# Gate/up bias loads on GpSimd's queue, the chunk count loaded once, and an output tail in quarters: a hybrid decoder step on one core

## What is computed

```python
x = x + merged @ w_out
hf = rmsnorm(x, g_ffn)
x = x + moe(hf, w_router, b_router, w_gu, b_gu, w_down, b_down)      # 32 experts, top 4
x = x + sigmoid(rmsnorm(x, g_ple) @ w_ple_gate) * (ple @ w_ple)

def expert(xblk, e):                        # D_FF = D_MODEL = 1024
    gu = xblk @ w_gu[e] + b_gu[e]           # 2 x 1024 columns: gate, up
    gate = minimum(gu[:, :D_FF], 7.0)
    up = clip(gu[:, D_FF:], -7.0, 7.0)
    hmid = (up + 1.0) * (gate * sigmoid(1.702 * gate))
    return hmid @ w_down[e] + b_down[e]
```

## Time and profile before

| | us |
|---|---|
| median of 3 runs | 1489.69 (1489.04 to 1493.76) |
| the profiled execution | 1497.59 |
| its span, first to last instruction | 1495.8 |
| TensorE busy in the span | 1403.3 (94%) |
| DVE, ACT, GpSimd busy | 420.1, 229.5, 18.5 |
| expert weights, 192 transfers of 2 MB | 19.2 each from issue to landing (median) |

### The profile page before, as it was taken

One profiled execution on the slowest core, in us unless ns is written; L12 is line 12 of the kernel. 1 busy time (PEld: TensorE's weight loads), 2 busy tenths in 40 slices (PEclk: granted clock), 3 DMA queues, 4 the chain that ended last, 5 costly groups with the idle time before them and its releaser, 6 DMA issues.

```text
span 1495.8 us, 17207 instructions
## 1 busy us (share of the span) xinstructions
PE 1403.3 (94%) x6990; PEld 704.0 (47%) x6990; DVE 420.1 (28%) x599; ACT 229.5 (15%) x383; POOL 18.5 (1%) x31
## 2 busy tenths in 40 slices
PE   7999996978899999999999999999999999999958
PEld 5887885864677433333333333333333333333327
DVE  2014944072313322222212221222122222212223
ACT  1113110241401311111111111111111111111001
POOL 0000000020000000000000000000000000000000
PEclk9999998998799999999999999999999999999979
DMA  9688899468663699999999999999999999999920
GB/s 381 270 334 280 297 338 367 163 215 248 268 250 120 269 394 429 429 428 428 428 429 428 430 427 428 428 429 427 429 428 428 430 428 429 428 428 428 425 109 30
DMA packets 42743, 530.37 MB, mean 355 GB/s; under 512 B 5981, under 2 KB 6125, under 8 KB 14261
## 3 DMA queue, kind: packets, MB, share of 16 engines
q1 hardware_dynamic: 39664, 470.69, 76.0%
q10 hardware_dynamic: 1685, 54.43, 9.6%
q0 software_dynamic: 1360, 4.76, 1.4%
HBM read 525.10 MB, written 58.38 MB: 390 GB/s over the span
## 4 chain that ended last, share of the span: by engine, by line
PE 71%; DMA 21%; DVE 3%; issue 2%; ACT 2%; SPq 1%; another core or an unknown queue 0%; DVEq 0%; ACTq 0%
PE PS L737 33%; DMA Zb<-in_b_gu 17%; PE PS L486 13%; DMA ring<-in_win 4%; PE PS L777 3%; PE PS L644 3%; PE PS L751 2%; PE PS L763 2%; PE PS L674 2%; PE PS L877 2%; PE PS L743 2%; PE PS L625 1%; ACT Zb L1045 1%; PE PS L497 1%; PE PS L529 1%
## 5 line engine op out<-in xcount | busy, mean ns | idle before, releaser
L737 PE MATMUL PS<-ring,Zb 128*64 128x512 f32 x3072 | 694.2, 601 | 0.9 <-ACT Zb L1019 0.5
L737 PEld LDWEIGHTS PS<-ring,Zb 128*64 128x64 f32 x3072 | 210.6, 138 | 405.2 <-issue 403.6
L486 PE MATMUL PS<-hT,ring 128*128 128x264 f32 x1024 | 233.7, 392 | 11.5 <-DMA ring<-in_win 11.5
L486 PEld LDWEIGHTS PS<-hT,ring 128*128 128x128 f32 x1024 | 197.8, 193 | 47.0 <-issue 12.3
L1364 DVE TENSOR_TENSOR xc<-xc,PS 128x528 f32<-128x528 f32 x132 | 92.5, 701 | 164.5 <-PE PS L777 153.9
L1392 DVE COPY Zb<-PS 128x512 f32<-128x512 f32 x32 | 22.1, 691 | 351.8 <-PE PS L737 351.8
L777 PE MATMUL PS<-Zb 64*128 64x264 f32 x512 | 92.2, 437 | 3.2 <-DVE xc L1364 2.4
L777 PEld LDWEIGHTS PS<-Zb 64*128 64x128 f32 x512 | 38.7, 185 | 105.9 <-issue 100.6
L1053 ACT ACTIVATE Zb<-Zb 128x512 f32<-128x512 f32 x32 | 20.2, 630 | 438.4 <-DVE Zb L1374 438.4
L1045 ACT ACTIVATE Zb<-PS 128x512 f32<-128x512 f32 x32 | 19.1, 597 | 350.2 <-PE PS L765 350.2
L751 PE MATMUL PS<-Zb 128*64 128x512 f32 x256 | 62.0, 605 | 0.0
(11 more groups left out here) (231 smaller groups left out, 898.3 us busy)
## 6 DMA issues: line engine op xcount, KB each, us to landing
ring<-in_wmoe SPq DMA_DIRECT2D x192, 2048.0 KB, 19.2
ring<-in_win SPq DMA_DIRECT2D x17, 2048.0 KB, 14.9
out_kvs<-in_cache ACTq DMA_DIRECT2D x8, 4032.0 KB, 25.1
out_kvs<-in_cache ACTq DMA_DIRECT2D x8, 1984.0 KB, 12.9
ring<-in_kt SPq DMA_DIRECT2D x2, 2048.0 KB, 14.5
ring<-in_cache SPq DMA_DIRECT2D x2, 2048.0 KB, 9.8
ring<-in_w_br_lru SPq DMA_DIRECT2D x2, 2048.0 KB, 20.3
ring<-in_w_out SPq DMA_DIRECT2D x2, 2048.0 KB, 16.0
```

What stands on the lines that cost most here:

```text
L486: last = mm(PS[:, t, 0:T], w[:, k, t * P:(t + 1) * P], hT[:, k, :], start=(k == 0), stop=(k == KT - 1))
L737: last = mm(PS[CAP * h:CAP * (h + 1), bank, :], src[:, k, f:f + CAP], w[:, k, h * CH:(h + 1) * CH], start=(slot == 4 and k == 0), stop=(sl ...
```

## The change

- The gate/up bias loads go from SP's queue to GpSimd's: the first waits for `bl_mm` as before, the others for `bias_used`. The six weight transfers of an expert stay as they are.
- Every engine, GpSimd now too, loads the token count once, early in the expert loop, and keeps it. Behind the loop stands one test for all further chunks; the spreads of the last expert in the old order, chunk 1, and the tests for chunks 2 to 4 are inside it. At its end DVE clears `yb`, and the others wait for that.
- The spreads of the last expert now follow the test. Their quarters use two pairs of PSUM banks in turn, so that the first two need no wait for an add. After each add DVE multiplies that quarter (row tiles j and j + 4) with the norm's gain, and TensorE adds its products to the first four column blocks, which are now built side by side in banks 4 to 7; the other four blocks follow one after the other. The squares are summed over the feature tiles on DVE by three halving adds, and TensorE sums over the partitions with one matmul, behind the first four blocks.
- SP stores the result in four pieces of 4, 2, 1 and 1 column blocks.

The diff, cut to its core:

```diff
+        def load_most(eng):
+            eng.wait_ge(S.cnt_ready, 1)
+            return eng.value_load(most, min_val=0, max_val=T)
+
+        def further(eng, count, block_of, first, last, before=None, after=None):
+            def chunk(c):
+                if before is not None:
+                    before(c)
+                with eng.Fori(0, E) as e:
+                    block_of(e, e + c * E)
+                if after is not None:
+                    after((c + 1) * E)
+            with eng.If(count > CAP):
+                first()
+                chunk(1)
+                for c in range(2, NCHUNK):
+                    with eng.If(count > c * CAP):
+                        chunk(c)
+                last()
...
+        def gate_up_bias(po, e, n):
+            po.wait_ge(S.bias_used, n)
+            po.dma_start(brow[0:64:32, :], a["b_gu"][e]).then_inc(S.brow_in, 16)
...
             def load(e, n):
-                sp.wait_ge(S.bias_used, n)
-                gate_up_bias(e).then_inc(S.brow_in, 16)
                 for s in range(6):
                     sp.wait_ge(used[s], n)
                     sp.dma_start(slot(s), weights(e, s)).then_inc(full[s], 16)
 
-            with sp.Fori(1, E) as e:
+            load(1, 1)
+            count = load_most(sp)
+            with sp.Fori(2, E) as e:
                 load(e, e)
-            sp.wait_ge(S.cnt_ready, 1)
-            further(sp, load, after=lambda n: sp.wait_ge(S.d1_mm, n))
+            further(sp, count, load, first=lambda: sp.wait_ge(S.d1_mm, E), last=lambda: sp.wait_ge(S.yb_zero, 1),
+                    after=lambda n: sp.wait_ge(S.d1_mm, n))
...
-            for half_ in range(2):
-                k = slice(4 * half_, 4 * half_ + 4)
-                sp.wait_ge(S.y_ok, 4 * half_ + 4)
-                sp.dma_start(a["yT"][:, k, :], sgp[:, k, :]).then_inc(S.out_done, 16)
+            for k0, k1 in ((0, 4), (4, 6), (6, 7), (7, 8)):
+                sp.wait_ge(S.y_ok, k1)
+                sp.dma_start(a["yT"][:, k0:k1, :], sgp[:, k0:k1, :]).then_inc(S.out_done, 16)
...
             block_(1)
+            count = load_most(pe)
             with pe.Fori(2, E - 1) as e:
                 block_(e)
             block_(E - 1, following=False)
-            spread_all(E - 1)
-            pe.wait_ge(S.cnt_ready, 1)
...
-            further(pe, apart, after=lambda n: pe.wait_ge(S.added, 4 * n + 4))
-            pe.wait_ge(S.h_ok, 2)
+            further(pe, count, apart, first=lambda: spread_all(E - 1), last=lambda: pe.wait_ge(S.yb_zero, 1),
+                    after=lambda n: pe.wait_ge(S.added, 4 * n + 4))
+            pe.wait_ge(S.added, 4 * E)
+            pe.wait_ge(S.u_rd, E)
+            pe.wait_ge(S.y_ev, E)
+            pe.wait_ge(S.goT_ok, E)
+            for j in range(4):
+                if j >= 2:
+                    pe.wait_ge(S.last_added, j - 1)
+                for h in range(2):
+                    last = mm(PS[:, 2 * ((j + 1) % 2) + h, 0:T], yb[CAP * h:CAP * (h + 1), j * P:(j + 1) * P],
+                              gpickT[CAP * h:CAP * (h + 1), :], start=True, stop=True)
+                last.then_inc(S.last_mm, 1)
             pe.wait_ge(S.wpg_in, 32)
-            for m in range(KT):
-                if m == 1:
-                    sum_sq(lt, 2)
-                if m >= 4:
-                    pe.wait_ge(S.pg_ev, m - 3)
+            for j in range(4):
+                pe.wait_ge(S.last_gain, j + 1)
+                for k in (j, j + 4):
+                    for m in range(4):
+                        last = mm(PS[:, 4 + m, 0:T], wpg[k // 4][:, k % 4, m * P:(m + 1) * P], hT[:, k, :],
+                                  start=(k == 0), stop=(k == 7))
+                        if k == 7:
+                            last.then_inc(S.pg_mm, 1)
+            pe.wait_ge(S.sq_ok, 2)
+            mm(PS[:, 0, 0:T], ones, lt[:, 0, :], start=True, stop=True).then_inc(S.ss_sum, 1)
+            for m in range(4, KT):
+                if m == 7:
+                    pe.wait_ge(S.rms_ok, 3)
                 for k in range(KT):
-                    last = mm(PS[:, m % 4, 0:T], wpg[k // 4][:, k % 4, m * P:(m + 1) * P], hT[:, k, :],
+                    last = mm(PS[:, (m - 3) % 4, 0:T], wpg[k // 4][:, k % 4, m * P:(m + 1) * P], hT[:, k, :],
...
+            v.wait_ge(S.added, 4 * E)
+            for j in range(4):
+                x = xc[:, :, :].rearrange("p (h k) t -> p h k t", h=2)[:, :, j, :]
+                hj = hT[:, :, :].rearrange("p (h k) t -> p h k t", h=2)[:, :, j, :]
+                gj = fv(FGP).rearrange("p (h k) t -> p h k t", h=2)[:, :, j, :]
+                b = 2 * ((j + 1) % 2)
+                v.wait_ge(S.last_mm, j + 1)
+                TT(x, x, PS[:, b:b + 2, 0:T], ALU.add).then_inc(S.last_added, 1)
+                v.wait_ge(S.last_added, j + 1)
+                TT(hj, x, gj, ALU.mult).then_inc(S.last_gain, 1)
+            link(TT(lt[:, :, :], xc[:, :, :], xc[:, :, :], ALU.mult))
+            for half_ in (4, 2, 1):
+                ins = TT(lt[:, 0:half_, :], lt[:, 0:half_, :], lt[:, half_:2 * half_, :], ALU.add)
...
             po.dma_start(xc[:, :, :], a["xT"]).then_inc(S.res_in, 16)
+            po.wait_ge(S.bl_mm, KT)
+            po.dma_start(brow[0:64:32, :], a["b_gu"][0]).then_inc(S.brow_in, 16)
+            gate_up_bias(po, 1, 1)
+            count = load_most(po)
+            with po.Fori(2, E) as e:
+                gate_up_bias(po, e, e)
+            further(po, count, lambda e, n: gate_up_bias(po, e, n), first=lambda: po.wait_ge(S.d1_mm, E),
+                    last=lambda: po.wait_ge(S.yb_zero, 1))
```

More of the change, by code:

```diff
@@ L217, in __init__ @@
         self.added = sem("added")
+        self.yb_zero = sem("yb_zero")
+        self.last_mm = sem("last_mm")
+        self.last_added = sem("last_added")
+        self.last_gain = sem("last_gain")
         self.wpg_in = sem("wpg_in")
@@ L417, in slot @@
                 return ring[:, s, :]
-            def gate_up_bias(e):
-                return sp.dma_start(brow[0:64:32, :], a["b_gu"][e])
             full = (S.w0, S.w1, S.w2, S.w3, S.w4, S.w5)
@@ L434, in _ @@
             sp.dma_start(slot(2), weights(0, 2)).then_inc(S.w2, 16)
-            gate_up_bias(0).then_inc(S.brow_in, 16)
             sp.dma_start(bdn, a["b_down"]).then_inc(S.bdn_in, 16)
@@ L456, in _ @@
             half(a["w_ple_gate"], 4, wpg[1], S.wpg_in)
-            for half_ in range(2):
-                k = slice(4 * half_, 4 * half_ + 4)
-                sp.wait_ge(S.y_ok, 4 * half_ + 4)
-                sp.dma_start(a["yT"][:, k, :], sgp[:, k, :]).then_inc(S.out_done, 16)
-            sp.wait_ge(S.out_done, 32)
+            for k0, k1 in ((0, 4), (4, 6), (6, 7), (7, 8)):
+                sp.wait_ge(S.y_ok, k1)
+                sp.dma_start(a["yT"][:, k0:k1, :], sgp[:, k0:k1, :]).then_inc(S.out_done, 16)
+            sp.wait_ge(S.out_done, 64)
             sp.wait_ge(S.kv_copy, 16 * (NS + 1) * NG)
@@ L1069, in _ @@
             ple_copy(7)
-            with act.Fori(0, E - 1) as e:
+            block_(0)
+            count = load_most(act)
+            with act.Fori(1, E - 1) as e:
                 block_(e)
             block_(E - 1, following=False)
-            act.wait_ge(S.cnt_ready, 1)
             def apart(e, n):
@@ L1078, in apart @@
                 block_(n, following=False)
-            further(act, apart)
-            root(3, rstd[:, :], PS[:, 4, 0:T], 1.0 / D).then_inc(S.rms_ok, 1)
+            further(act, count, apart, first=lambda: act.wait_ge(S.y_ev, E), last=lambda: act.wait_ge(S.yb_zero, 1))
+            root(3, rstd[:, :], PS[:, 0, 0:T], 1.0 / D).then_inc(S.rms_ok, 1)
             for m in range(KT):
@@ L1396, in _ @@
             block_(0, 0)
+            count = load_most(v)
             with v.Fori(1, E - 1) as e:
@@ L1399, in _, with add_last @@
             block_(E - 1, E - 1, following=False)
-            for j in range(4):
-                add_spread(E - 1, j)
+            def add_last():
+                for j in range(4):
+                    add_spread(E - 1, j)
             def shift_ranks(c):
@@ L1414, in apart @@
                     add_spread(n, j)
[L1416 to L1419, removed]
+            further(v, count, apart, first=add_last, last=lambda: nc.vector.memset(yb, 0.0).then_inc(S.yb_zero, 1),
+                    before=shift_ranks, after=lambda n: v.wait_ge(S.added, 4 * n + 4))
+            v.wait_ge(S.added, 4 * E)
+            for j in range(4):
+                x = xc[:, :, :].rearrange("p (h k) t -> p h k t", h=2)[:, :, j, :]
[9 more added lines that the diff above has]
+                ins = TT(lt[:, 0:half_, :], lt[:, 0:half_, :], lt[:, half_:2 * half_, :], ALU.add)
+                if half_ > 1:
+                    link(ins)
+            ins.then_inc(S.sq_ok, 1)
             v.wait_ge(S.rms_ok, 3)
@@ L1430, in _ @@
                 v.wait_ge(S.pg_mm, m + 1)
-                TT(sgp[:, m, :], PS[:, m % 4, 0:T], rstd[:, :], ALU.mult).then_inc(S.pg_ev, 1)
```

(1 more changed line is left out.)

## The result

| | median us | runs | ratio to before (95%) |
|---|---|---|---|
| before, beside the first runs | 1491.72 | 4 (1489.04 to 1495.14) | |
| after | 1467.68 | 4 (1466.03 to 1469.60) | 0.9842 (0.9824 to 0.9860) |
| after, run again with the experiments | 1469.23 | 4 (1468.16 to 1470.69) | 0.9854 (0.9839 to 0.9869) |

The change saves 24.0 us in the first comparison and 22.4 in the second; 21.4 were forecast (1468.3 us). The profiled execution of after took 1466.88 us, span 1465.2.

A forecast was written before the change was run, and what follows sets the result against it. DMA was taken to bound the late expert rounds, with one engine about 8 us behind, TensorE the early ones. Gate product 17.4, sum of squares 3.1 and store 0.9 made 21.4 us: 1489.69 to 1468.3 us, range 1458 to 1475.

The forecast's parts named there:

- The loop: Expert loop: bias wait goes, weights are late next; last down product 3.0 us earlier, at 1432.2; bounds 0 to 10.
- The laggard: One DMA engine about 8 us behind, with every weight transfer waiting for it; forecast to stay after the bias move.
- GpSimd's queue: Bias loads there land after 5.4 us, even 20 hidden; rival: they land late, 1541 us, 3%.
- Count loaded once: Early load of the token count on the engines: costs nothing, at worst 0.55 us.
- The gate product hangs on the landing: Tail: first gate matmul follows w_ple_gate's second half, at 1438.3 instead of 1455.69: 17.4 us.
- One branch: TensorE's test ahead of the last spreads, reached 4.5 us before the last down product ends; dearest took 3.7: hidden.
- 3 us of slack: Tail: further margin for the branch beyond 4.5 us; first gain quarter stands at 1435.2, w_ple_gate lands at 1438.2.
- the rival's 15 us: Rival: one TensorE branch costs what the four did, about 15 us; gate matmul at 1445, total 1475 us; 8%.
- Sum of squares and store: Tail: one matmul replaces eight, saving 3.1 us; smaller last store saves 0.9 us, bounds 0 to 1.3.
- The first block: First gate column block kept at 6.02 us after a clock fall; 2.5 us less with none, 1 more if longer.
- the cure: Rival: GpSimd's queue spreads the bias rows and the slow DMA engine catches up; 1461 us; 27%.

The follow-up runs named there:

- tail alone: The changed kernel with the bias loads back on SP's queue, ahead of each expert's six weights: 1470.59 us, ratio 0.9849.
- biases at once: The changed kernel with all 32 biases loaded ahead of the expert loop, none in it, seeds using a one-hot selector: 1461.18 us, ratio 0.9791.
- old sum and stores: The changed kernel with the sum of squares as eight TensorE matmuls again and the result stored in two pieces: 1473.36 us, ratio 0.9877.
- bias move alone: The kernel before with the bias loads on GpSimd's queue and the old tail: 1488.69 us, ratio 0.9975.

## Why the prediction was right, point by point

**The loop: right.** The bias wait went and the weights are late in its place; the last down product ends at 1425.8 + 6.8 = 1432.6 (forecast 1432.2). The laggard stayed: 29.68 us a round after, 29.67 before. The reason held as well, and one row costs 0.16 us where 0.15 was argued from one engine's 27 GB/s; the gap that the prediction read as 0.25 us is 29.68 - 29.37 = 0.31, both rows on one engine. The Trainium skill's "DMA: Bandwidth & Descriptors", "The descriptor swizzle", puts partitions 0 to 3 and 32 to 35 behind one port and 64 to 67 and 96 to 99 behind another. The pitches agree with it: 29.53 us with a row behind each, 29.74 with two and two, 30.00 with four behind the first. The rule that spoke for the cure (the Trainium skill, same page, "Why a DMA increments its semaphore by 16 and not by 1") is about which engines carry a transfer; no run here shows that, and the pitch did not change with the queue.

**GpSimd's queue: right.** The biases landed in 5.5 us (5.4 taken). That 20 would have been hidden too was argued and not tried.

**Count loaded once: right.** It was put at nothing, and TensorE's early rounds stayed at 28.48 us. No run tries it alone.

**The gate product hangs on the landing: right.** 1431.72 + 6.8 = 1438.5, forecast 1438.3: the 17.4 us. That this "does not hang on the loop" is borne out in time (tail alone 0.9849, all 0.9842 and 0.9854), but not in its working: the prediction let the first quarter alone release the product and overlooked the fourth spread ahead of it in TensorE's order. In the tail-alone kernel that put the gate product 2.95 us behind the landing (1439.15 against 1436.2). In the changed kernel it stays hidden, by the 1.3 us above.

**One branch: right, with less to spare than the working had.** It took 4.15 us with a lead of 3.9 (4.5 taken), and the copy behind the last product covered what was left. The "3 us of slack" behind it were 1.3, since the fourth spread, not the first quarter, is what stands ahead of the gate product. The same test took TensorE 3.35 us (tail alone) to 6.07 us (biases at once) in the kernels here, where the four had taken 3.7 at most; at 5.17, in the kernel with the old sum and stores, 0.2 us of the wait for the landing was left. So a branch of this kind was hidden by a narrow margin, while the rival's 15 us were far from anything seen.

**Sum of squares and store: right.** 3.1 us and 0.9 us, each read off when put back. In the kernel before the end after the last matmul took 5.6 us, some 0.4 more than with the old stores put back; where that comes from is open.

**The first block: mis-sized, within its bounds.** The prediction kept a clock fall of 2.5 us. The first 64 gate matmuls took 14.51 us in one execution of after and 16.19 in another, where 6.02 + 10.68 = 16.70 had been put down; 0.5 to 2.2 us of the gain are here, most of what lies beyond the forecast (2.6 us in the first comparison, 1.0 in the second). TensorE was not "nearly off" in the pause: the spreads kept it busy for 2.59 of the 5.95 us between the last product and the gate product. That this is why the clock held is not shown.

## What to carry to other kernels

Where a loop is bound by DMA, look at the last landing and not at the mean rate: a transfer of a few KB a round that always goes to the same partitions held back every weight transfer behind it, 0.16 us for each 4 KB of a round and some 6 to 8 us in all (1467.68 against 1461.18 us; 0.9842 against 0.9791 of the kernel before). Another queue cured nothing, the two rows in places apart (partitions 0 and 96) halved it, and one load for all rounds removed it. Read a branch's cost on the engine that takes it, and lay the common case out as the fall-through (0.08 us where the taken branch had 3.35 to 6.07). When a product is made to wait for a transfer, list what else stands ahead of it in its engine's order, since that is what becomes late once the transfer is early.

## What was not expected of the hardware

- Three small matmuls on different rows of TensorE ran at a time (L778, L779 and L780 of a round in about 1.1 us), and moving one of them onto another's rows added 0.83 us a round (0.93 against 0.10).
- The same taken branch on TensorE took from 3.35 to 6.07 us in kernels that differ little there, yet 4.15 and 4.13 in two executions of the same kernel; one that fell through took 0.08 us, and on DVE the same test took 0.06. What sets it is open.
- The clock after the same short pause differed between two executions of the same kernel: 14.51 and 16.19 us for the same 64 matmuls, at 1.00 and 0.89. In the profile of after the loop had a granted clock of 1.00 throughout, where before had 0.98 in the late rounds. That goes with the bias: from 900 to 1350 us it was 0.98 with the tail alone (bias on SP) and 1.00 with the bias move alone. Why is open.
